# Second layer's token blocks: one-hot products from rows kept on the chip in place of indirect gathers, and the next layer's small parameters issued by GpSimd

## What is computed

```python
for l in range(DEPTH):            # DEPTH = 2
    ...                           # adaLN, norm, one input projection, four head groups, output projection
    m_x = modulate(rms_norm(x, g_norm2[l]), sh2, sc2)
    if last:
        x = x + ga2 * hier_moe(m_x, *moe_p)
    else:
        y = hier_moe(concatenate([m_x, m_c]), *moe_p)
        ...
return rms_norm(x, g_final)

def run_block(e, toks):           # inside hier_moe
    xb = h[toks]
    gt, up = split(xb @ w_in[e], 2)
    return (silu(gt) * up) @ w_out[e]
```

## Time and profile before

| | us |
|---|---|
| three executions | 1418.17, 1424.20, 1423.37 |
| their median | 1423.37 |
| the profiled execution, device time | 1419.92 |
| its span, first to last instruction | 1418.1 |
| second layer's mixing part begins | about 790 |
| second layer's expert loop, on TensorE | 972.6 to about 1407 |

### The profile page before, as it was taken

The page is one execution under the profiler, slowest core; times in us unless marked ns, Lnnn a source line. Parts: engine busy times, 40 slices in busy tenths (PEclk is TensorE's granted clock), DMA queues, the critical chain, the costliest instruction groups (busy, mean ns, idle before and its releaser), DMA issues.

```text
span 1418.1 us, 31382 instructions
## 1 busy us (share of the span) xinstructions
PE 1181.9 (83%) x12641; PEld 647.9 (46%) x12642; DVE 589.6 (42%) x1341; ACT 202.5 (14%) x431; POOL 202.5 (14%) x364
## 2 busy tenths in 40 slices
PE   6999999998989999776998799997888766666565
PEld 3446454554545554333554684554444433333232
DVE  2491163376767776544776541544111100100102
ACT  3104310520000000000000324131000000000001
POOL 3005011021111111101111020111111101101100
PEclk9999999999999999989999999998999988888887
DMA  9712663989999989999999545788999999999995
GB/s 335 279 59 88 248 238 117 356 302 412 422 420 416 406 338 421 420 418 423 419 417 415 205 168 207 282 346 309 418 416 377 419 419 421 421 418 422 421 416 236
DMA packets 107160, 485.38 MB, mean 342 GB/s; under 512 B 9975, under 2 KB 28995, under 8 KB 91122
## 3 DMA queue, kind: packets, MB, share of 16 engines
q1 hardware_dynamic: 99442, 472.05, 83.2%
q0 software_dynamic: 5648, 8.99, 1.8%
q10 hardware_dynamic: 2032, 3.82, 0.8%
HBM read 485.90 MB, written 4.23 MB: 346 GB/s over the span
## 4 chain that ended last, share of the span: by engine, by line
PE 50%; SPq 23%; DMA 13%; DVE 5%; issue 5%; ACT 3%; POOL 0%; DVEq 0%; ACTq 0%; POOLq 0%
SPq L813 21%; PE bank L1711 10%; DMA ring<-in_expert_w_out 7%; PE bank L1405 7%; PE bank L1736 6%; PE bank L1586 6%; DMA work<-in_expert_w_out 5%; PE bank L1726 5%; PE bank L1506 4%; PE bank L1301 3%; DVE resid L1832 2%; PE bank L1422 2%; ACT msb L1031 1%; PE bank L1717 1%; PE bank L1472 1%
## 5 line engine op out<-in xcount | busy, mean ns | idle before, releaser
L1711 PE MATMUL bank<-ring,msb 128*32 128x256 f32 x3456 | 226.9, 407 | 75.5 <-DMA ring<-in_expert_w_in 54.6
L1832 DVE TENSOR_TENSOR resid<-bank,resid 128x512 f32<-128x512 f32 x384 | 238.0, 682 | 120.0 <-PE bank L1736 120.0
L1031 ACT ACTIVATE msb<-bank 128x256 f32<-128x256 f32 (+2 forms) x190 | 69.2, 364 | 906.6 <-PE bank L1711 811.6
L1711 PEld LDWEIGHTS bank<-ring,msb 128*32 128x32 f32 x3456 | 109.1, 115 | 183.2 <-DMA ring<-in_expert_w_in 70.9
L2120 DVE COPY msb<-bank 128x256 f32<-128x256 f32 x85 | 35.6, 419 | 269.3 <-PE bank L1675 269.1
L1726 PE MATMUL bank<-ring,msb 128*32 128x256 f32 x1728 | 112.2, 403 | 36.6 <-DMA ring<-in_expert_w_out 28.3
L992 POOL COPY work<-work 128x256 f32<-128x256 f32 x86 | 34.4, 400 | 685.2 <-issue 353.8
L1736 PE MATMUL bank<-work 32*128 32x256 f32 x1376 | 109.4, 436 | 4.6 <-DVE msb L2143 4.0
L982 POOL DMA_INDIRECT work<-h_rows,gidx x86 | 88.7, 1031 | 73.9 <-POOL gidx L979 73.0
L1405 PE MATMUL bank<-actT,ring 128*128 128x256 f32 (+1 forms) x320 | 97.2, 465 | 0.5 <-ACT actT L1087 0.5
L1726 PEld LDWEIGHTS bank<-ring,msb 128*32 128x32 f32 x1728 | 56.1, 114 | 80.9 <-issue 34.5
(11 more groups left out here) (273 smaller groups left out, 1116.6 us busy)
## 6 DMA issues: line engine op xcount, KB each, us to landing
ring<-in_expert_w_in SPq DMA_DIRECT2D x82, 2048.0 KB, 30.6
ring<-in_expert_w_out SPq DMA_DIRECT2D x41, 2048.0 KB
ring<-in_w_mod SPq DMA_DIRECT2D x24, 2048.0 KB, 8.7
actT<-in_expert_w_in SPq DMA_DIRECT2D x21, 2048.0 KB
states<-in_expert_w_in SPq DMA_DIRECT2D x21, 2048.0 KB, 30.6
work<-in_expert_w_out SPq DMA_DIRECT2D x21, 2048.0 KB
ring<-in_w_in SPq DMA_DIRECT2D x7, 2048.0 KB, 11.9
ring<-in_w_out SPq DMA_DIRECT2D x4, 2048.0 KB, 8.6
```

The costliest lines, as they stand in the source:

```text
L1031: return act.activation(o, i, func, **kw)
L1711: ins = mm(PS[1][q, 0:256], xeT[:, c % 2, BLK * (c // 2):BLK * (c // 2 + 1)], w[:, k, 256 * g:256 * (g + 1)], start=c == 0, stop=c == KT - 1)
L1832: ins = tt(v, PS[4 + g].rearrange("p (t n) -> p t n", t=2), v, ALU.add)
```

## The change

In the second layer no row is stored to HBM or gathered. `htok` lies in the context half of the residual stream, `X[:, 2:, :]`, which that layer no longer needs after its second norm. Every block but the first is made in the loop: VectorE compares the rows' positions with the slot numbers of the block after next (`picked`, then `picks`), TensorE multiplies `picks` with `htok` between `scatter(0)` and `hidden(1)` (8 products into the unused half of PSUM bank 3), and ScalarE copies the result to `xs`. GpSimd's part in that loop is gone. The 23 small DMAs move from SP's queue to GpSimd, at the end of the first layer's loop. The orders `ahead` and the waits for the slots 6 and 7 change.

```diff
-    jobs += [(("next", 3), "A")] * more + [(("first", 0), ""), (("first", 1), "")]
+    jobs += [(("next", 3), "A")] * more + [(("first", 0), "")] + [(("first", 1), "")] * more
...
-        htok = states[:, 0:4096].rearrange("p (t d) -> p t d", t=TILES)
+        htoks = [states[:, 0:4096].rearrange("p (t d) -> p t d", t=TILES), X[:, XT_TILES:, :]]
+        picks = work[:, 0:BLK * XT_TILES].rearrange("p (t s) -> p t s", t=XT_TILES)
+        picked = work[:, 256:256 + 2 * BLK * XT_TILES].rearrange("p (j t s) -> p j t s", j=2, t=XT_TILES)
...
+            if not more:
+                tt(picks, mine[0][:, 0:nt, BLK:2 * BLK], mine[1][:, 0:nt, BLK:2 * BLK], ALU.add).then_inc(b_picks[l], 1)
...
                 if l + 1 < DEPTH:
-                    ahead = (0, 1), (0, 0), (0, 2), (2, 1), (1, 0), (2, 0), (2, 2), (1, 1), (1, 2)
+                    ahead = (0, 1), (0, 0), (0, 2), (2, 1), (2, 0), (1, 0), (2, 2), (1, 1), (1, 2)
                 else:
-                    ahead = (0, 0), (2, 0), (0, 1), (0, 2), (2, 1), (2, 2), (1, 0), (1, 1), (1, 2)
+                    ahead = (0, 0), (2, 0), (0, 1), (1, 1), (0, 2), (2, 2), (2, 1), (1, 0), (1, 2)
...
-                    elif s == 4:
+                    elif s == 4 or s == 6 and l + 1 == DEPTH:
                         sp.wait_ge(made, jobs.at[(l, "o", LAYER_T[l] - 1)] + 1)
...
                     elif s == 6:
-                        got(sp, "D", l, "routerT")
-                        if l + 1 < DEPTH:
-                            load_modulation(sp, l + 1)
-                            load_params(sp, l + 1)
                         sp.wait_ge(s_hd, 16 * sum(LAYER_T[:l + 1]))
                         sp.wait_ge(made, jobs.at[(l, "first", 1)] + 1)
                     else:
-                        sp.wait_ge(made, jobs.at[(l, "tables")] + 1)
-                        sp.wait_ge(s_tab, l + 1)
+                        got(sp, "D", l, "tables")
...
+                if l + 1 == DEPTH:
+                    pool.memset(ye[0], 0.0).then_inc(b_ye[l], 1)
+                    pool.memset(sel, 0.0).then_inc(b_sel[l], 1)
+                    pool.sem_inc(s_gend, 1)
+                    continue
...
                 pool.sem_inc(s_gend, 1)
+                got(pool, "D", l, "routerT")
+                load_modulation(pool, l + 1)
+                load_params(pool, l + 1)
...
+                    if l + 1 == DEPTH:
+                        act.wait_ge(b_g[l], k + 1)
+                        copy(xs, PS[3][:, QTR:2 * QTR]).then_inc(b_xs[l], 1)
                     act.wait_ge(b_hid[l], k + 1)
                     copy(raw, PS[1][:, 0:256]).then_inc(b_raw[l], 1)
...
                         scatter(0, not whole).then_inc(b_scA[l], 1)
+
+                        if whole:
+                            got(pe, "D", l, "tables")
+                            pe.wait_ge(b_picks[l], k + 1)
+                            for t in range(nt):
+                                for g in range(4):
+                                    q = slice(BLK * g, BLK * (g + 1))
+                                    ins = mm(PS[3][q, QTR:2 * QTR], picks[:, t, :], htok[:, t, QTR * g:QTR * (g + 1)],
+                                             start=t == 0, stop=t == nt - 1)
+                            ins.then_inc(b_g[l], 1)
...
                     ins.then_inc(b_ye[l], 1)
+                    if whole:
+                        stt(picked.rearrange("p j t s -> p (j t) s"), bc(const("slot")[:, 0:BLK], 1, 2 * nt), const("rows_ahead")[:, bass.ds(k, 1)],
+                            bc(pos_all[:, 0:2 * nt], 2, BLK), ALU.add, ALU.is_equal).then_inc(b_pick[l], 1)
+                        dve.wait_ge(b_pick[l], k + 1)
+                        tt(picks, picked[:, 0, :, :], picked[:, 1, :, :], ALU.add).then_inc(b_picks[l], 1)
```

More of the change, by code:

```diff
@@ L76, in _const_layout @@
                     ("tok1", TILES), ("qrow", 1), ("rev4", NG), ("rev32", NE), ("thr", 2 * 16), ("expert", 1),
-                    ("before32", NE), ("slot", P), ("block", MAX_BLOCKS), ("inv", 2 * POOL_N)):
+                    ("before32", NE), ("slot", P), ("block", MAX_BLOCKS), ("rows_ahead", MAX_BLOCKS), ("inv", 2 * POOL_N)):
         CONST_COLS[name] = (at, n)
@@ L422, in build @@
         wt = sm(2 * TILES).rearrange("p (j t) -> p j t", j=2)
[L423 removed]
+        pos_all = sm(2 * TILES)
         cnt = sm(17)
@@ L445, in build @@
         s_in = [sem("x_loaded"), sem("ctx_loaded")]
-        s_mpar = sem("modulation_params_loaded")
+        s_mpar = [sem(f"modulation_params_loaded{l}") for l in range(DEPTH)]
         s_par = [sem(f"params_loaded{l}") for l in range(DEPTH)]
@@ L491, in build @@
             [sem(f"b_{n}{l}") for l in range(DEPTH)] for n in b_names]
+        b_pick, b_picks, b_g = [[sem(f"b_{n}{l}") for l in range(DEPTH)] for n in ("pick_terms", "picks", "rows_picked")]
         b_gath = [[sem(f"b_gathered{l}_{b}") for b in range(2)] for l in range(DEPTH)]
@@ L1241, in _ @@
                     quarter_rows(l, 3, "next")
-                act.wait_ge(s_pool, xg_clear[l])
-                for b in range(2):
-                    bank = take(act, l, "first", b)
-                    copy(xg[:, b, :], bank[:, 0:QTR]).then_inc(s_xg, 1)
+                if l + 1 < DEPTH:
+                    act.wait_ge(s_pool, xg_clear[l])
+                    for b in range(2):
+                        bank = take(act, l, "first", b)
+                        copy(xg[:, b, :], bank[:, 0:QTR]).then_inc(s_xg, 1)
+                else:
+                    copy(xs, take(act, l, "first", 0)[:, 0:QTR]).then_inc(b_xs[l], 1)
                 act.wait_ge(s_xt, l + 1)
@@ L1661, in _ @@
                 pe.wait_ge(s_first, l + 1)
-                for b in range(2):
+                htok = htoks[l]
+                for b in range(2 if l + 1 < DEPTH else 1):
                     bank = open_(l, "first", b)
@@ L1697, in _ @@
                 ins.then_inc(made, 1)
-                pe.wait_ge(s_xg, 2 * l + 2)
+                if l + 1 < DEPTH:
+                    pe.wait_ge(s_xg, 2)
                 for c, s in (("A", read_a), ("D", read_d)):
```

31 lines of the change are left out of this document (18 added, 13 removed).

## The result

| | before | with the change |
|---|---|---|
| median of 20 executions each, us | 1420.06 | 1424.23 |
| lowest to highest | 1417.26 to 1424.20 | 1421.12 to 1426.77 |
| profiled execution, device time | 1419.92 | 1424.47 |
| its span | 1418.1 | 1422.4 |

The ratio is 1.0028 with the 95% interval [1.0020, 1.0037]: some 4 us longer, a slowdown that is clear of the scatter but smaller than the 0.5% that the prediction took as its bound. A slowdown beyond that bound was the likeliest forecast (0.55). The median of before, measured with more executions, is itself 3.3 us lower than the median of three that the prediction had.

What follows compares the result with a forecast made beforehand. TensorE was taken to bound the second loop up to 1082 us, the DMAs after that. Six terms summed to +7.9 us: 1427.8 or 1431.3 us by base, the middle 1429.5 us forecast, range 1420 to 1437.5 us.

Steps and rivals of the forecast that it cites:

- term 3: Second loop's DMA-bound part: the gathers being gone saves 1.8 us, ends 0.3 and 2.6 us.
- Term 1: Second loop up to 1082 us: eight more products per block, twelve blocks at 0.97 us, +11.6 us.
- Terms 4 and 5: Parameter DMAs off SP's queue save 4.1 us in the first loop; issued on GpSimd at its end they cost 1.2 us.
- term 5: End of the first layer: parameter DMAs on GpSimd take from the weights' stream, +1.2 us, ends 0 and 2.8.
- Term 2: Start of the second loop: one small sum more in VectorE's routing chain, +0.2 us, between -1.0 and +1.0.
- Term 6: Last block: the eight products partly covered by the wait for weights, +0.8 us, ends 0 and 2.5.
- signs given for a right step: What the profile after should show, such as 10.0 us blocks in the second loop and first-layer loads some 9 us earlier.
- A: Rival: the DMAs bound the whole second loop, so the products cost nothing; 1415 us, not slower, chance 0.12.
- B: Rival: rows come late in second-loop blocks up to 1082 us, 7 us more, 1437 us, chance 0.12.
- C: Rival: the first layer gives nothing, -4.1 us becomes 0, 1433.6 us, chance 0.08.
- D: Rival: second layer as forecast, but start, gathers and end all fall well; +3.1 us, 1424.7 us, chance 0.18.
- the hole: Second loop's last dip in DMA share, ended by a refill at 1082 us; forecast deeper and about 8 us later.

Runs made afterwards that it cites:

- e3: Kernel before with the second layer's gathers in the loop left out (blocks from the third on work on old rows): 1414.14 us, ratio 0.9956.
- e4: Kernel before with the second layer's gathers kept but every row skipped, so they move nothing: 1416.59 us, ratio 0.9981.
- e5: The change with each block's eight products done twice in the same place: 1432.66 us, ratio 1.0092.
- e10: The change itself, unaltered, measured again in a later session: 1423.58 us, ratio 1.0024.
- e2: Kernel before with only the 23 parameter DMAs moved to GpSimd at the end of the first loop: 1418.48 us, ratio 0.9983.
- e7: Kernel before with only the first layer's load order changed, chunk (2, 0) ahead of (1, 0): 1416.58 us, ratio 0.9974.
- e12: The change with the second layer's first loads in the order of before: 1423.03 us, ratio 1.0020.

## Why the prediction was wrong

The mechanisms were the right ones and the kernel did get slower, but the sum was +7.9 us, the measurement about +4, and the likeliest case was a slowdown beyond 0.5% where 0.28% came out. (The forecast time of 1429.5 us lay 5.3 us high. 1.5 us of that is its base, 1421.6 us, where the median of before is now 1420.06 us. The other 3.7 us, 3.9 by the ratio, are the sum, and that is what is explained here.)

**The step that failed is term 3, the gathers at -1.8 us.** They were worth -5.8 us in the traces (rate and tail), and e3 without them was 5.7 to 6.2 us faster, with 6.9 us less in its trace's stretch. The prediction had three prices: 0.3 us from two rates of SP's queue, 1.8 us by bytes, 2.6 us by the queue's own share, and took the middle. All three were too low, so the true value lay outside the ends. The comparison of rates misled most: it set 417.3 GB/s beside 417.7 GB/s in a stretch where the gathers carried 0.00 MB, and took that stretch for one without gathers. But its row has 144 packets on that queue. The last gathers run ahead of the blocks that are left and skip nearly all of their rows, and e4 shows that such DMAs cost the weights' stream 419.2 against 421.9 GB/s. Nowhere in the DMA-bound part of before did this loop run without them, so the price could not be read there. A stretch of 35 us is also too short for a price of 1%: e3, with no gather at all, moved 14.60 MB in the same window, no more than the 14.62 MB of before, and from 14.58 to 14.93 MB in other windows of 35 us. The share of 0.8% was the packets' own time, and the stream lost 1.2% of its rate, 3.7 us. The last 2 us are the tail behind 1380 us, of which the prediction had no notion. With 5.8 in place of 1.8 the sum is 11.6 + 0.2 - 5.8 - 4.1 + 1.2 + 0.8 = +3.9 us, which is what was measured. That it fits so well is luck: the products came out 2.2 us below their term and the boundary 1.9 us above its own, and about half of both is the clock at two places of these two traces.

**Term 1, the products, +11.6 us:** measured +9.4 us in the traces, 10.3 us of trace and some 9 us of time for a second set (e5). The number of blocks was right. 0.9 of the missing 2.2 us are the clock in the first block, which was lower in before and differs between traces of one kernel too (8.00 us for that block in the change, 9.34 us in e10). Counted from the first `back` the products cost 9.5 us in eleven blocks, 10.4 us for twelve. The rest is the size. A set takes 0.86 us and not 0.97: the row of 3.92 us for 32 products was read as busy time, which holds the fill of the last one and was not a start-to-start time; `hidden`'s 1.87 us for 16 in the loop was the nearer row, and a set stands 0.89 us before the next instruction. The lower end, 11.2 us, was too high as well, even against 10.4 us.

**Terms 4 and 5, the first layer, -4.1 and +1.2 us:** the size is right (-3.8 us at the refill; in time, -2.4 us by e2's ratio and -1.3 by its medians, for both terms), the cause only half. The prediction priced `ahead` at nothing, without naming what hides it. It would have had -3.3 us by itself (e7) and does the same work as the move of the parameters. The rows showed it: the load for (2, 0) went out right behind the one to `actT`, at 287.14 us, with its slot long free. On the other side of the boundary the traces have +2.2 us between the last `back` and the next layer's first products, of which 1.3 us are that `back` at the lower clock. It did not come again in e10 (11.7 us there, 13.5 in the change, 11.3 before), and kernels with the parameters on either queue spread over the same range, so it is not charged to them. What they do cost is the 0.9 us ahead of it, near the 1.2 us of term 5. The rule of the Trainium skill that was weighed there (DMA: Bandwidth & Descriptors, Queues, rings and completion order), by which small packets go in turn with the weights, would have made the sum 1.6 us larger. The weights' queue did move less while the parameters went out, which fits the rule, but the cost stayed at 0.9 us and not near the upper end of 2.8. For the gathers it fits what e3 and e4 show: a queue with little to move still took from the stream.

**Term 2, start of the loop, +0.2 us:** measured +0.1. **Term 6, the end, +0.8 us:** measured +1.4 us, none of it the products themselves (`back` waits 2.06 us for its weights, more than before), all of it the clock: 3.32 us against 1.93 us for `back`. e10, the same kernel, has 2.78 us there, so this too is partly scatter.

**The rivals.** A (the DMAs bound the whole loop) is out: the third column of the table. B (rows late) is out: 1.7 us of cover, no wait before the products. C (first layer gives nothing) is out: the refill came 3.8 us earlier and the waits were gone. D came nearest in time, 3.1 against 4 us, but by another way: the gathers fell better than thought, and further than D allowed, the products lay below its 11.2 us, and the start and the end did not fall well. Of the signs given for a right step, the block's length (9.04 to 9.9 us at a change of expert, 10.0 forecast), no idle time before the products, the loads to the last slots earlier (12 us, 9 forecast), the waits for weights gone and the earlier refill came true; the hole came 9.4 us later in the loop, and 8.7 us later in the trace.

## What to carry to other kernels

Work that is added to an engine on the critical path should go where that engine already waits: the same eight products cost 10 us behind the scatter and 2 us or less before `back`, and one block more of lookahead pays for the move. A stretch with 0.00 MB on a queue is a stretch without that queue's cost only if its packet count is zero as well, and it must be long enough that its own scatter is below the price sought; the price of small DMAs beside a saturated stream is read from the stream's rate with and without them. And in a queue that issues in order, look for a load whose slot is free behind one whose slot is not: swapping two entries gave as much here as moving 23 DMAs.

## What the runs showed of the hardware

- Gathers that skip all of their rows still cost a saturated stream of 2 MB loads: 419.2 GB/s beside them, 421.9 GB/s without, 417.1 GB/s with rows of 0.72 MB in 280 us (e4, e3, before). The time that the record puts on their packets, 0.2% and 0.8%, is less than what the stream loses against e3, 0.6% and 1.1%. With real gathers the stream also ended some 2 us less well filled, in three kernels of three, though the gathers moved no row in that stretch (before, e2, e7).
- 23 small DMAs with 0.43 MB, issued by GpSimd beside the weights' stream, took 7.2 to 7.3% of the engines' time over 22 us, and the layer's last `back` came 0.9 us later (seven traces against seven).
- A set of eight one-hot products shows 1.07 us of busy time and takes 0.89 us of the engine's, start to start; twice the set takes 1.93 and 1.75 us.
- After a wait for weights of over 2 us, `back` ran for 3.25 and 3.32 us in the change at both places, with granted clocks of 0.59 and 0.60; after 1.26 and 1.33 us (before) for 1.93 us. It isn't a firm line: `back` took 1.93 us after waits of 2.01 us (e5, boundary), 2.16 us (e12, boundary) and 2.14 us (e7, end), and 3.10 us after one of 1.80 us (the change, the last but one) and 2.78 us after 1.73 us (e10, end). So a microsecond or two at a loop's end or start come and go with the clock.
